# A hybrid decoder step on Trainium2: norms made chunk by chunk inside the projection that follows

## The reference, cut to what matters

```python
def rmsnorm(x, g):
    xf = x.astype(jnp.float32)
    y = xf * lax.rsqrt(jnp.mean(xf * xf, -1, keepdims=True) + RMS_EPS)
    return (y * g).astype(x.dtype)

# layer
#   rmsnorm(x, attn_norm) @ w_in  -> RWKV-7 columns | NSA columns | gates
#   RWKV-7 mixing and NSA attention in parallel, merged, output projection, + x
#   rmsnorm(x, ffn_norm)  @ peer_wq -> product-key expert retrieval, + x
#   rmsnorm(x, ple_norm)  @ ple_w_gate -> sigmoid, times p @ ple_w_in, + x
```

## Time and profile before

| | us |
|---|---|
| median of 3 runs (lowest to highest) | 2946.91 (2941.17 to 2950.7) |
| the profiled execution's own time | 2951.34 |
| its span | 2949.5 |
| PE busy | 2561.9 (87%) |
| DVE busy | 1444.1 (49%) |
| ACT busy | 1023.9 (35%) |

### The profile page before, as it was taken

The page is one execution under the profiler, slowest core; times in us unless marked ns, Lnnn a source line. Parts: engine busy times, 40 slices in busy tenths (PEclk is TensorE's granted clock), DMA queues, the critical chain, the costliest instruction groups (busy, mean ns, idle before and its releaser), DMA issues. The chain is left out here.

```text
span 2949.5 us, 51892 instructions
## 1 busy us (share of the span) xinstructions
PE 2561.9 (87%) x20580; PEld 2163.3 (73%) x20580; DVE 1444.1 (49%) x3144; ACT 1023.9 (35%) x1811; POOL 887.5 (30%) x782
## 2 busy tenths in 40 slices
PE   6984886798966898799999987799999999999959
PEld 5983875587534887699999977676777777777738
DVE  3354442422754323449999955344443444444442
ACT  2112110122542120124444466544444444444531
POOL 0000000000000000001111264477777777777710
PEclk8986997798786999899999999899999999999979
DMA  3210000332301211135555534799999999999932
GB/s 110 84 34 6 4 12 29 111 110 69 104 6 61 85 61 65 53 107 188 182 184 186 180 135 170 268 349 343 351 347 344 348 345 331 343 351 344 347 119 68
DMA packets 207162, 511.44 MB, mean 173 GB/s; under 512 B 32099, under 2 KB 99171, under 8 KB 205475
## 3 DMA queue, kind: packets, MB, share of 16 engines
q1 hardware_dynamic: 150626, 340.46, 33.7%
q0 software_dynamic: 56320, 167.98, 15.8%
HBM read 463.91 MB, written 48.56 MB: 174 GB/s over the span
## 5 line engine op out<-in xcount | busy, mean ns | idle before, releaser
L2230 POOL TENSOR_TENSOR wide<-wide,sif 128x2048 f32<-128x2048 f32 (+1 forms) x10 | 52.7, 5266 | 1627.7 <-DVE wide L2346 1627.7
L2480 POOL DMA_INDIRECT dots<-dots,place x320 | 371.0, 1159 | 128.1 <-issue 97.2
L2484 POOL DMA_INDIRECT v_row<-in_peer_v,expert x320 | 361.8, 1131 | 97.6 <-issue 97.6
L2615 DVE TENSOR_TENSOR v_lo<-v_raw,v_hi 128x1024 fp32r<-128x1024 f32 x128 | 156.9, 1226 | 392.5 <-ACT v_hi L2564 392.5
L2095 PE MATMUL ps<-h_hi,u_hi 128*128 128x320 f32 x1024 | 320.9, 313 | 10.2 <-DVE u_lo L2252 10.2
L2095 PE MATMUL ps<-h_lo,u_hi 128*128 128x320 f32 x1024 | 317.1, 310 | 0.0
L2095 PE MATMUL ps<-h_hi,u_lo 128*128 128x320 f32 x1024 | 317.1, 310 | 0.0
L2506 PE MATMUL ps<-h_hi,u_hi 128*128 128x256 f32 x1024 | 299.3, 292 | 11.4 <-DVE u_lo L2610 11.4
L2506 PE MATMUL ps<-h_lo,u_hi 128*128 128x256 f32 x1024 | 291.0, 284 | 0.0
L2506 PE MATMUL ps<-h_hi,u_lo 128*128 128x256 f32 x1024 | 290.7, 284 | 0.0
L2506 PEld LDWEIGHTS ps<-h_hi,u_hi 128*128 128x128 f32 x1024 | 196.4, 192 | 86.0 <-issue 69.4
(11 more groups left out here) (471 smaller groups left out, 5251.1 us busy)
## 6 DMA issues: line engine op xcount, KB each, us to landing
u_raw<-in_peer_u SPq DMA_DIRECT2D x256, 512.0 KB
v_raw<-in_peer_v SPq DMA_DIRECT2D x128, 512.0 KB, 5.9
dots<-dots SPq DMA_DIRECT2D x128, 160.0 KB, 1.8
g<-gate_matrix SPq DMA_DIRECT2D x32, 512.0 KB, 7.9
wt<-in_w_in SPq DMA_DIRECT2D x24, 512.0 KB, 3.5
pages<-in_cmp_pages SPq DMA_DIRECT2D x64, 128.0 KB, 2.0
kv_pages<-in_sel_pages SPq DMA_DIRECT2D x64, 128.0 KB, 2.0
wt<-in_w_zg SPq DMA_DIRECT2D x16, 512.0 KB, 3.5
```

Of the source, the lines that this page charges most:

```text
L2230: nc.gpsimd.tensor_tensor(hot4, hot4, which, ALU.mult).then_inc(numbered, 1)
L2480: nc.gpsimd.indirect_dma_start(dots[:, s:s + 1], None, dots_flat, bass.IndirectOffsetOnAxis(f.place[:, s:s + 1], 0)).then_inc(d_got[s % SL ...
L2484: nc.gpsimd.indirect_dma_start(v_row(s), None, v_rows, bass.IndirectOffsetOnAxis(f.expert[:, s:s + 1], 0)).then_inc(v_got[s % SLOTS], 16)
L2615: nc.vector.tensor_tensor(v_lo[:, j % 2], v_raw[:, j % RV], v_hi[:, j % 2].bitcast(F32), ALU.subtract).then_inc(v_parted, 1)
```

## The change

`norm_stage` goes. A new class, `NormTiles`, holds the three steps of a normed chunk (`scale` on DVE, `round` on ACT, `rest` on DVE) with three buffers in a ring, and `project_stage` and `embed_stage` call them one chunk at a time. The first two weight tiles are multiplied chunk by chunk along with that: TensorE waits for chunk c of `h_lo`, multiplies it with chunk c of the gate columns (site 1), of tile 0 and of tile 1, then takes chunk c+1. `w_hi` of tiles 0 and 1 moves from DVE to ACT (in `embed_stage` it is there already), between the first `round` steps. The loads of the first weight tiles are now the first thing in the projection's block, with the gate columns behind tile 0. The loops of `project_stage` are written out. From tile 2 on the work is as before.

```diff
-def norm_stage(k, gain, hi, lo, ring):
...
+class NormTiles:
...
+        self.own = k.sb(ctx, "normed", [P, 3, T])
...
+    def scale(self, dve, c):
+        if c >= 3:
+            dve.wait_ge(self.lowered, c - 2)
+        self.k.nc.vector.scalar_tensor_tensor(out=self.own[:, c % 3, :], in0=self.k.x[:, c, :], scalar=self.k.par(self.gain, c),
+                                              in1=self.k.rs[:], op0=ALU.mult, op1=ALU.mult).then_inc(self.normed, 1)
+    def round(self, act, c):
+        act.wait_ge(self.normed, c + 1)
+        self.k.nc.scalar.activation(self.hi[:, c, :], self.own[:, c % 3, :], ACT.Copy).then_inc(self.rounded, 1)
+    def rest(self, dve, c):
+        dve.wait_ge(self.rounded, c + 1)
+        self.k.nc.vector.tensor_tensor(self.lo[:, c, :], self.own[:, c % 3, :], self.hi[:, c, :].bitcast(F32),
+                                       ALU.subtract).then_inc(self.lowered, 1)
# project_stage, vector
+            def split(n):
+                if n >= 2:
+                    dve.wait_ge(arrived[n % ring], 16 * (n // ring + 1))
+                    dve.wait_ge(multiplied, n - 1)
+                    nc.vector.tensor_copy(w_hi[:, n % 2], wt[:, n % ring]).then_inc(rounded, 1)
+                dve.wait_ge(rounded, n + 1)
...
+            norm.scale(dve, 0)
+            norm.scale(dve, 1)
+            norm.rest(dve, 0)
...
+            split(0)
+            norm.scale(dve, 2)
+            norm.rest(dve, 1)
+            split(1)
+            for c in range(2, KD):
+                if c + 1 < KD:
+                    norm.scale(dve, c + 1)
+                norm.rest(dve, c)
# project_stage, tensor
+            for c in range(KD):
+                pe.wait_ge(norm.lowered, c + 1)
+                if gates is not None:
+                    if c == 0:
+                        pe.wait_ge(gate_parted, 1)
+                    gate(c)
+                for n in range(2):
+                    if c == 0:
+                        pe.wait_ge(parted, n + 1)
+                    tile(n, c)
+            for n in range(2, ntiles):
+                pe.wait_ge(parted, n + 1)
...
# project_stage, scalar
+            norm.round(act, 0)
+            for c in range(1, KD):
+                if c <= 2:
+                    act.wait_ge(arrived[c - 1], 16)
+                    nc.scalar.activation(w_hi[:, c - 1], wt[:, c - 1], ACT.Copy).then_inc(rounded, 1)
+                norm.round(act, c)
# embed_stage, tensor
+            for c in range(KD):
+                pe.wait_ge(norm.lowered, c + 1)
+                for n in range(2):
+                    if c == 0:
+                        pe.wait_ge(parted, n + 1)
+                    gate(n, c)
+            pe.wait_ge(loaded, 16)
+            value(0)
+            value(1)
```

More of the change, by code:

```diff
@@ new lines, in _ @@
+            for c in range(2, KD):
+                if c + 1 < KD:
+                    norm.scale(dve, c + 1)
+                norm.rest(dve, c)
+            todo = [] if shift is None else [(12, 13)] + [(n, n + 1) for n in range(0, 12, 2)]
+            if todo:
+                dve.wait_ge(prev_in, 16)
+            for n in range(2, ntiles):
+                split(n)
+                if todo and n >= RCOLS + 2:
+                    last = shift_two(todo.pop(0))
+            assert not todo
+            if shift is not None:
@@ L403, in _ @@
[L403 to L413, removed]
@@ L414, in _, with tile @@
-            if gates is not None:
-                pe.wait_ge(gate_rows, 1)
-                pe.wait_ge(taken, ntiles + 1)
+            def tile(n, c):
+                for m, (lhs, r) in enumerate(three_passes(w_hi[:, n % 2, c, :], w_lo[:, n % 2, c, :], r_hi, r_lo)):
+                    for h in range(2):
+                        mm = nc.tensor.matmul(k.bank(2 * (n % ring) + h, TH), lhs, r[:, c, h * TH:(h + 1) * TH],
+                                              start=c == 0 and m == 0, stop=c == KD - 1 and m == 2)
+                if c == KD - 1:
+                    mm.then_inc(multiplied, 1)
@@ new lines, in gate @@
+            def gate(c):
+                for n, (lhs, r) in enumerate(three_passes(g_hi[:, c, :], g_lo[:, c, :], r_hi, r_lo)):
+                    for h in range(2):
+                        mm = nc.tensor.matmul(k.ps[0:NGATE, 6 + h, 0:TH], lhs, r[:, c, h * TH:(h + 1) * TH],
+                                              start=c == 0 and n == 0, stop=c == KD - 1 and n == 2)
+                if c == KD - 1:
+                    mm.then_inc(gate_mm, 1)
+            for c in range(KD):
+                pe.wait_ge(norm.lowered, c + 1)
+                if gates is not None:
+                    if c == 0:
[5 more added lines that the diff above has]
+                    tile(n, c)
@@ L419, in _ @@
+            for n in range(2, ntiles):
+                pe.wait_ge(parted, n + 1)
+                if n == 3 and gates is not None:
+                    pe.wait_ge(gate_rows, 1)
+                if n >= ring:
+                    pe.wait_ge(taken, n - ring + 1)
+                for c in range(KD):
+                    tile(n, c)
+            if gates is not None:
+                pe.wait_ge(taken, ntiles - ring + 1)
                 for tt in range(5):
@@ L426, in _ @@
         def _(act):
[L427 to L430, removed]
+            norm.round(act, 0)
[4 more added lines that the diff above has]
+                norm.round(act, c)
+            if gates is not None:
                 act.wait_ge(gate_mm, 1)
                 nc.scalar.activation(halves(g_rows[:]), k.ps[0:NGATE, 6:8, 0:TH], ACT.Copy).then_inc(gate_rows, 1)
[L433 to L439, removed]
+            for n in range(ntiles):
+                act.wait_ge(multiplied, n + 1)
+                nc.scalar.activation(halves(dst[:, n, :]), k.pair(2 * (n % ring)), ACT.Copy).then_inc(taken, 1)
             if gates is not None:
@@ L2735, in _, with gate, value @@
         def _(pe):
[L2736 to L2745, removed]
+            def gate(n, c):
+                for m, (lhs, r) in enumerate(three_passes(w_hi[:, n % 2, c, :], w_lo[:, n % 2, c, :], *h)):
+                    for s in range(2):
+                        nc.tensor.matmul(k.bank(4 * (n % 2) + s, TH), lhs, r[:, c, s * TH:(s + 1) * TH],
+                                         start=c == 0 and m == 0, stop=c == KD - 1 and m == 2)
+            def value(n):
                 for c in range(2):
@@ L2769, in _, with low @@
             ch = Chain(dve, chain)
-            for n in range(KD + 1):
-                if n < KD:
-                    dve.wait_ge(rounded, n + 1)
-                    nc.vector.tensor_tensor(w_lo[:, n % 2], wt[:, n % ring, 0:KD, :], w_hi[:, n % 2].bitcast(F32),
-                                            ALU.subtract).then_inc(parted, 1)
+            def low(n):
+                dve.wait_ge(rounded, n + 1)
+                nc.vector.tensor_tensor(w_lo[:, n % 2], wt[:, n % ring, 0:KD, :], w_hi[:, n % 2].bitcast(F32),
+                                        ALU.subtract).then_inc(parted, 1)
+            norm.scale(dve, 0)
+            norm.scale(dve, 1)
+            norm.rest(dve, 0)
+            low(0)
+            norm.scale(dve, 2)
+            norm.rest(dve, 1)
+            low(1)
+            for c in range(2, KD):
+                if c + 1 < KD:
+                    norm.scale(dve, c + 1)
+                norm.rest(dve, c)
+            for n in range(1, KD + 1):
+                if 2 <= n < KD:
+                    low(n)
                 if n:
```

99 lines of the change are left out of this document (44 added, 55 removed).

## The result

| | before | after |
|---|---|---|
| median of 17 runs, us | 2945.74 | 2935.38 |
| lowest to highest, us | 2939.77 to 2952.09, and one execution of 6368.10 | 2926.93 to 2944.92 |
| ratio (95% interval) | | 0.9966 (0.9955 to 0.9977) |
| span of the profiled execution, us | 2949.5 | 2931.4 |

The kernel became 10 us faster, where 23 were forecast: right in direction, wrong in size, and 0.4 us outside the range of 2914 to 2935. The changed kernel was compared with the one before twice more in this study, and the ratio came out at 0.9965 and 0.9968, so the size is not chance.

What follows compares the result with a forecast made beforehand. Each projection was taken as bound by TensorE, leaving the wait before its first multiplication to win; site gains of 7.1 + 5.5 + 5.5 + 5.8 = 23.9, with clock terms taken as 23, gave 2924 us, range 2914 to 2935.

Steps and rivals of the forecast that it cites:

- The start: TensorE's first multiplication at each site: 4.5 (site 1), 6.2 (sites 2, 3) and 7.2 us (site 4) behind the block's start.
- The hole at tile 1: New TensorE standstill at each site until `w_lo` of tile 1 is ready: about 1.1 us, 1.15 at site 1.
- The hole at tile 2: New TensorE standstill at each site until `w_lo` of tile 2 is ready: 1.5 us, 1.6 at site 4.
- the rival in which this hole costs the clock: Clock falls at tile 2, each site losing 2.25 us more: gain 14, time 2933; chance 0.13.
- The clock at the start: Sites' first multiplications: low-clock loss 0.55 us less than now or, at sites 2 and 3, 0.7 more; middle taken.
- The sum of the sites: Gains of 7.1, 5.5, 5.5 and 5.8 us at sites 1 to 4: 23.9, with ends of 20.4 and 26.15.
- what is won is passed on whole, if no later wait takes it back: Ends of the four sites' blocks: all engines meet there, so the sites' gain reaches the whole kernel.
- the entry of the written-out loops among the edits at nothing: Projection loops written out: no gain, as 24 tiles in 153.7 us leave no room, and no charge for straight code.
- The rival that gave straight code a cost: Projections' 48 tiles: fresh code starves TensorE 0.4 us per tile, 19 us in all; gain 4, time 2943; chance 0.05.
- The prediction's own last sign of being wrong: Stages behind the change: the prediction is wrong if a later stage starts with a longer wait than now.

Runs made afterwards that it cites:

- c_looped: The changed kernel with the projections' tiles from 4 on back in loops of 4 on all engines; 2934.83 us, ratio 0.9965 to the kernel before.
- f_pool_pad: The changed kernel with 9 more instructions on GpSimd (fulfilled waits and a branch) in the load stage; 2930.83 us, ratio 0.9959 to the kernel before.
- i_looped_pad: The changed kernel with projection tiles from 4 on in loops and GpSimd's filler in the load stage; 2934.24 us, ratio 0.9963 to the kernel before.
- o_pe_only_131: The kernel before with TensorE's projection loop written out and 131 more TensorE instructions in site 3's norm stage; 2950.41 us, ratio 1.0024.
- n_before_pe131: The kernel before, loops kept, with 131 more instructions on TensorE in the norm stage of site 3; 2956.91 us, ratio 1.0044.

## Why the prediction was right on the sites and wrong on the whole

**The start.** Forecast 4.5, 6.2 and 7.2 us behind the block's start; measured 4.6 at site 1, 6.2 and 6.1 at sites 2 and 3, and 6.5 at site 4, where the first tile landed after 4.0 us and not 4.7. Right.

**The hole at tile 1.** Forecast 1.1 us; measured 0.66 idle at sites 2 to 4 and 1.80 at site 1. (The forecast counted from issue to issue, the profile from the modelled end; from issue to issue site 2 has 0.9.) At site 1 ACT waited for `w1` until 27.71, 7.15 us behind the block's start, and the forecast had it landed 5.1 us behind it: behind the gate columns it came 2 us later, and the split of tile 1 was done 1 us later.

**The hole at tile 2.** Forecast 1.5 and 1.6; measured 1.37, 1.31, 1.33 and 1.52 idle. The clock stayed high behind each of them, in the three profiles of the changed kernel and in those of c_looped, f_pool_pad and i_looped_pad too. So the rival in which this hole costs the clock did not come true at any site. Its 2933 lies near the measured 2935 by chance.

**The clock at the start.** The middle of two ends was taken: a rise 4.5 us behind the first multiplication, or 4.5 behind the restart, which is 7. At site 1 it came before tile 1's first multiplication (0.53 at 30.08); at site 2 that multiplication took 0.85, so it was later. Over sites 1 to 3 in three profiles the granted clock rose 3.6 to 8.7 us behind the first multiplication, so the two ends were too narrow. This is also why site 3 gave 5.7 us in one profile and 4.2 in the next: the rise came after 5.3 us in the first and after 8.7 in the second, and half of the 3.4 us more at the low clock is 1.7, which covers the 1.5 us lost.

**The sum of the sites.** 23.9 forecast, with ends of 20.4 and 26.15; 24.3 in the first profile. Over the three profiles of the changed kernel against that of before it is 24.3, 21.4 and 22.0. Right.

**The step that failed** is the sentence that "what is won is passed on whole, if no later wait takes it back", and with it the entry of the written-out loops among the edits at nothing. That the loops cost and give nothing at the sites was right: 24 tiles take the same time either way. But the edit moved all later code in the instruction streams, and the price was looked for only where the code was changed. The rival that gave straight code a cost put it there too, at TensorE's tiles in the projections. The prediction's own last sign of being wrong came true: a later stage, that of the experts, starts with a longer wait, 5.5 us for `dots` against 3.8. What the runs showed in place of the 23 us passed on whole:

- GpSimd's standstill, 3.1 to 3.5 us, in all five profiles with the norm stages gone and GpSimd's stream not filled up, and in none of the others. Shown: filler removes it, and `start` is 3 us shorter. That it is an instruction fetch rests on timing: an 8 KB packet of instructions arrives in it in all five, and in none of the other 13 profiles at this place. The total of a kernel did not show the 3 us: c_looped with and without the standstill takes the same time. It stands one gather behind a branch, while the DMA engines are loaded; the Trainium skill (Runtime: NRT & Kernel Launch, section Instruction fetch mechanics) says that a taken branch breaks the sequential prefetch, and the prediction weighed this rule only for the loops, where the trace left it nothing.
- The place in TensorE's stream moves `main` by some 7 to 12 us, in both directions by the same filler. With it moves the time at which TensorE's packets of instructions arrive, and the longest waits for `dots` are longer where such a packet comes 3 to 7 us ahead of their end. What the packet delays is open. The last link is seen: over the 18 profiles each microsecond of low clock in `main` goes with half a microsecond of its length (correlation 0.82; before: 4.0 us of low clock, 910.2; o_pe_only_131: 6.8, 912.1; n_before_pe131: 24.3, 922.3; the changed kernel: 18.2, 919.3). It is no rule for a single wait. The clock fell behind some of 1.9 us and stayed high behind others of 3.3 and 3.6, and f_pool_pad, with its packets in the late place and a wait of 3.3 us, has the third shortest `main`, 912.3.
- For the changed kernel itself this cause is likely but not isolated. Its packets lie in the late place and its longest waits are 3.7, 4.5 and 3.7 us, but no run moved them back, with its norms made chunk by chunk, to where they were. Its `main` was 919.3, 917.8 and 915.7, against 910.2 to 914.9 in four profiles with TensorE's code where it was before: in means 917.6 against 913.3, 4.3 us. With 2.5 us for `start` (35.6 against 33.1) and 22.6 for the sites this leaves 16 us; measured are 10, with an interval of 7 to 13. Of the 6 us between, 4 are the choice of executions: the four profiled ones with TensorE's code in its old place ran 2.2 to 6.9 us above the medians of their kernels, the three of the changed kernel 0.4 above theirs in the mean. So the profiles, taken as they are, agree with 16, and what is left open against the medians is about 2 us, less than their noise.

## What to carry to other kernels

Feeding a matmul chunk by chunk while its operand is being made won at the sites what their rows promised, and the doubled operand should be staggered, one tile some chunks behind the other: otherwise both tiles end together and the split of the next has no cover. After an edit that changes the number of instructions, look at stages that were not touched; here it was one near two bounds at once, and a difference of 0.3% came from there. The time at which instruction packets arrive in such a stage can be read from the trace, and compared before and after. Before believing a small gain or loss, run a control that moves the code and changes no work.

## What was not expected of the hardware

Fulfilled waits are not free: some 250 more instructions of them (490 waits) on an engine that had nothing to do made the load stage 4 us longer, and 131 (254 waits) on TensorE made site 3 3.5 us longer, since 24.7 us passed there before its first multiplication instead of 21.2. In the kernel before, 131 such instructions on TensorE made `main` of a stage that begins 650 us later 9 to 12 us longer. And the packets of instructions, which a profile counts among its DMA queues, show up in the times of other engines' work, although they are 0.3 to 0.4% of what the DMA engines do.
